# Routing of a two-layer trunk's mixture of experts rebuilt: router in strips, placement on GpSimd, expert rows fetched from DRAM, loops written out

## The reference

```
h = rms_norm(x);  q|k|v|value|gate = h @ w_in[layer]
attention: 8 heads, window 128, sinks;   conv: GLU, causal width 31, layer norm, silu
x = x + concat(attention, conv) @ w_out[layer]
h = rms_norm(x)
layer 0:  x = x + (silu(h @ w_gate) * (h @ w_up)) @ w_down          # width 2816
layer 1:  logits = h @ w_router                                      # 8 experts
          top 2 of 8 experts per token, softmax over the two logits
          x = x + sum over the two of weight * (silu(h @ w_gate[e]) * (h @ w_up[e])) @ w_down[e]   # width 3584
```

## Time and profile before

| | us |
|---|---|
| median of 3 runs | 1451.32 (1450.49 to 1452.38) |
| the profiled execution | 1446.28 |
| its span, first to last instruction | 1444.7 |
| PE busy | 1372.9 (95%) |
| DVE busy | 1076.3 (74%) |
| ACT busy | 915.5 (63%) |
| POOL busy | 53.7 (4%) |

### The profile page before, as it was taken

One profiled execution on the slowest core, in us unless ns is written; L12 is line 12 of the kernel. 1 busy time (PEld: TensorE's weight loads), 2 busy tenths in 40 slices (PEclk: granted clock), 3 DMA queues, 4 the chain that ended last, 5 costly groups with the idle time before them and its releaser, 6 DMA issues.

```text
span 1444.7 us, 19503 instructions
## 1 busy us (share of the span) xinstructions
PE 1372.9 (95%) x7441; PEld 1162.3 (80%) x7442; DVE 1076.3 (74%) x715; ACT 915.5 (63%) x731; POOL 53.7 (4%) x77
## 2 busy tenths in 40 slices
PE   6998999989988999999999999999999999999994
PEld 5867999979667888888788888878888888888883
DVE  5555444553656888888888898888888888888883
ACT  4564434344554777767776777767677677777771
POOL 3220000010200000000000000000000000000001
PEclk9999999989988999999999999999999999999997
DMA  9545655643624999999999999999999999999992
GB/s 323 157 138 170 202 174 181 211 145 108 206 88 145 368 342 363 393 370 336 372 378 339 376 386 340 343 392 368 339 373 392 343 372 390 358 355 382 390 343 103
DMA packets 198951, 428.10 MB, mean 296 GB/s; under 512 B 9304, under 2 KB 45392, under 8 KB 198864
## 3 DMA queue, kind: packets, MB, share of 16 engines
q1 hardware_dynamic: 195392, 416.71, 80.6%
q0 software_dynamic: 3472, 10.21, 1.9%
HBM read 415.42 MB, written 6.82 MB: 292 GB/s over the span
## 4 chain that ended last, share of the span: by engine, by line
PE 90%; DVE 4%; ACT 2%; DMA 1%; issue 1%; SPq 0%; POOL 0%; POOLq 0%; ACTq 0%; DVEq 0%
PE ps L1006 88%; DVE w_low L728 2%; PE ps L1209 2%; ACT w_high L514 1%; DMA raw<-in_w_in 1%; DMA raw<-y_slots,row_i 0%; PE ps L1029 0%; DVE hT_both L751 0%; SPq L344 0%; DVE h_td L744 0%; PE ps L1117 0%; DVE work_b L776 0%; DVE mx L769 0%; DVE h_td L833 0%; ACT sc L585 0%
## 5 line engine op out<-in xcount | busy, mean ns | idle before, releaser
L728 DVE TENSOR_TENSOR w_low<-raw,w_high 128x2048 fp32r<-128x2048 f32 x391 | 896.3, 2299 | 232.1 <-ACT w_high L514 231.6
L514 ACT ACTIVATE w_high<-raw 128x2048 fp32r<-128x2048 f32 x391 | 749.2, 1917 | 267.3 <-PE ps L1006 263.3
L1006 PE MATMUL ps<-w_high,hT_both 128*128 128x512 f32 (+1 forms) x1920 | 602.8, 391 | 13.2 <-issue 5.9
L1006 PEld LDWEIGHTS ps<-w_high,hT_both 128*128 128x128 f32 x1920 | 361.5, 189 | 86.9 <-issue 11.4
L1006 PE MATMUL ps<-w_low,hT_both 128*128 128x512 f32 (+1 forms) x960 | 372.2, 388 | 0.0
L1006 PE MATMUL ps<-w_high,act_both 128*128 128x512 f32 x1072 | 342.9, 391 | 1.8 <-DVE act_both L909 1.8
L1006 PEld LDWEIGHTS ps<-w_high,act_both 128*128 128x128 f32 x1072 | 202.2, 189 | 43.7 <-DVE act_both L909 2.1
L1006 PEld LDWEIGHTS ps<-w_low,hT_both 128*128 128x128 f32 x960 | 182.1, 190 | 35.0
L1006 PE MATMUL ps<-w_low,act_both 128*128 128x512 f32 x536 | 209.4, 391 | 0.0
L1006 PE MATMUL ps<-hT_both,w_high 128*128 128x256 f32 x960 | 177.5, 285 | 2.6 <-DVE hT_both L751 2.6
L1006 PEld LDWEIGHTS ps<-hT_both,w_high 128*128 128x128 f32 x960 | 152.1, 193 | 3.8 <-DVE hT_both L751 2.8
(11 more groups left out here) (184 smaller groups left out, 582.7 us busy)
## 6 DMA issues: line engine op xcount, KB each, us to landing
raw<-in_moe_w_gate SPq DMA_DIRECT2D x112, 1024.0 KB, 7.2
raw<-in_moe_w_up SPq DMA_DIRECT2D x112, 1024.0 KB, 7.2
raw<-in_moe_w_down SPq DMA_DIRECT2D x112, 1024.0 KB, 6.9
raw<-in_w_in SPq DMA_DIRECT2D x14, 1024.0 KB, 7.0
raw<-in_dense_w_gate SPq DMA_DIRECT2D x11, 1024.0 KB, 5.3
raw<-in_dense_w_up SPq DMA_DIRECT2D x11, 1024.0 KB, 5.4
raw<-in_dense_w_down SPq DMA_DIRECT2D x11, 1024.0 KB, 4.9
raw<-in_w_out SPq DMA_DIRECT2D x8, 1024.0 KB, 6.8
```

Source lines behind the costliest of these rows:

```text
L514: act.activation(w_part[0][:, s % PART_RING, :], raw[:, s % RAW_RING, :], ACT.Copy).then_inc(w_high_done, 1)
L728: dve.tensor_tensor(w_part[1][:, q, :], raw[:, r, :], w_part[0][:, q, :], ALU.subtract).then_inc(w_low_done, 1)
L1006: return pe.matmul(out_, lhsT, rhs, start=start, stop=stop, skip_group_check=True)
```

## The change

Five parts.

1. Norms 1, 2 and 3 treat block 1 in two halves of 512 columns. The last projection slot finishes the first half 6 matmuls early and says so (`half_projected`). ACT's sum of block 1 takes three activations before the root instead of one, and the weight slots that ACT rounded between the transposes are rounded after them. PE's first dense matmuls wait for the k chunks one pair at a time.
2. Router: `wr` is padded to 32 columns and is the stationary operand; 8 matmuls of 256 columns go to four column strips of the array, ACT copies the four partial results, and 2 matmuls with `mask` add them and turn them back. `route` loses an addition and two copies, the one-hot of experts 1 to 7 goes, and the weights' part (`weigh`) moves to DVE's end.
3. Placement runs on POOL (28 small instructions, each waiting for the one before). POOL writes `h_td` to DRAM, scatters the token numbers into a list with 4 indirect transfers, reads it back, and before each of experts 1 to 7 fetches its 128 rows (512 KB) to `xrows`. PE turns them by 8 transposes (`turn_rows`) where `gather` stood. Expert 0 is still gathered by matmuls.
4. The loop over expert pairs is written out on all engines.
5. The number of overflow passes is read at each engine's end.

```diff
-            with pe.Fori(0, NE // 2 - 1) as i:
-                expert_steps(S_MOE + 4, 0, 0, 2, True, i, (PAIR, 2 * EG, 2), lambda k: i * 2 + k)
-            expert_steps(S_MOE + 4 + (NE // 2 - 1) * PAIR, (NE - 2) * EG, NE - 2, 2, False, None, (0, 0, 0), lambda k: NE - 2 + k)
+            expert_steps(S_MOE + 4, 0, 0, NE, False, None, (0, 0, 0))
...
+            def turn_rows(i, per, e):
+                pe.wait_ge(rows_read, at(i, 16 * per, 16 * e))
+                for j in range(2):
+                    for k in range(4):
+                        last = pe.transpose(ps[:, (3, 6)[j], k * P:(k + 1) * P], xrows[:, (4 * j + k) * P:(4 * j + k + 1) * P], ident[:, :])
+                    last.then_inc(gathered, 1)
...
-                            gather(i, per_e, e + k // EG + 1, e_reg(k // EG + 1))
+                            turn_rows(i, per_e, e + k // EG + 1)
...
+            for i in range(2):
+                for g in range(4):
+                    last = mm(ps[QUAD * g:QUAD * (g + 1), 4, 0:S], wr[:, 4 * i + g, :], hT_plain[:, 4 * i + g, :], i == 0, i == 1)
+            last.then_inc(routed, 1)
+            pe.wait_ge(lgT_ready, 1)
             for t in range(NB):
-                for k in range(KC):
-                    last = mm(ps[:, 4, t * NE:(t + 1) * NE], hT_plain[:, k, t * P:(t + 1) * P], wr[:, k, :], k == 0 and t == 0, k == KC - 1)
-            last.then_inc(routed, 1)
+                last = mm(ps[:, 5, t * NE:(t + 1) * NE], lgT[:, t * P:(t + 1) * P], mask[:, 0:NE], True, True)
+            last.then_inc(summed, 1)
...
+            mm(ps[:, 4, NE:2 * NE], ones[:, :], sel[:, 0, :], False, True).then_inc(counted, 1)
+            mm(ps[:, 7, 0:NE], ones[:, :], sel[:, 0, :], True)
+            mm(ps[:, 7, 0:NE], ones[:, :], sel[:, 1, :], False, True).then_inc(counted, 1)
...
+                            if first and m == 0 and f == 0 and k % 2 == 0:
+                                pe.wait_ge(hT_low_done, 4 + k // 2 + 1)
...
+            act.wait_ge(routed, 1)
+            act.activation(lgT, ps[:, 4, 0:S], ACT.Copy).then_inc(lgT_ready, 1)
             act.wait_ge(zdiff_done, 1)
...
-            n_passes = passes_in_all(act)
             act.wait_ge(w_used, S_MOE + 2)
             act.activation(silu_t, ps[:, 0, :], ACT.Silu).then_inc(silu_done, 1)
...
-            place()
-            n_passes = passes_in_all(dve)
             dve.wait_ge(w_used, S_MOE + 4)
...
+                    act.wait_ge(x_added, 3 * (q - 1) + 2)
+                    act.activation(h_td[:, 1, 0:D // 2], xr[:, 1, 0:D // 2], ACT.Square, accum_out=ss[:, q, 1:2]).then_inc(sq_done, 1)
+                    act.wait_ge(sq_done, done + 2)
+                    act.activation(ss_half[:, q, 0:1], ss[:, q, 1:2], ACT.Identity, scale=1.0 / D, bias=eps_t[:, :]).then_inc(sq_done, 1)
+                    act.wait_ge(x_added, 3 * (q - 1) + 3)
+                    act.activation(h_td[:, 1, D // 2:D], xr[:, 1, D // 2:D], ACT.Square, accum_out=ss_half[:, q, 1:2]).then_inc(sq_done, 1)
+                    act.wait_ge(sq_done, done + 4)
+                    act.activation(rms[:, q, 1:2], ss_half[:, q, 1:2], ACT.Sqrt, scale=1.0 / D, bias=ss_half[:, q, 0:1]).then_inc(rms_done, 1)
...
+            for b in range(NB):
+                pool.wait_ge(h_done, 9 + 2 * b + 1)
+                pool.dma_start(h_dram[b * P:(b + 1) * P, :], h_td[:, b, :]).then_inc(h_stored, 16)
+            list_tokens()
+            place()
+            pool.wait_ge(h_stored, 16 * NB)
+            def fetch(e):
+                pool.wait_ge(gathered, 2 * e)
+                pool.indirect_dma_start(out=xrows[:, :], out_offset=None, in_=h_dram[:, :],
+                                        in_offset=bass.IndirectOffsetOnAxis(ap=slot_tok[:, e:e + 1], axis=0)).then_inc(rows_read, 16)
...
-            with pool.Fori(0, NE) as e:
+            for e in range(NE):
+                if e + 1 < NE:
+                    fetch(e + 1)
                 store(e)
+            n_passes = passes_in_all(pool)
```

More of the change, by code:

```diff
@@ L472, in conv, with link, add_up @@
                 pool.dma_start(gnorm[:, 1, :], ffn_norm_g[l].partition_broadcast(P)).then_inc(gain_loaded[1], 16)
+            steps = [0]
+            def link(ins):
+                steps[0] += 1
+                ins.then_inc(place_step, 1)
+                pool.wait_ge(place_step, steps[0])
+            def add_up(total, t):
+                for n in (4, 2):
+                    link(pool.tensor_tensor(t[..., 0:n], t[..., 0:n], t[..., n:2 * n], ALU.add))
+                link(pool.tensor_tensor(total, t[..., 0], t[..., 1], ALU.add))
@@ L534, in norm @@
                         act.activation(hT_plain[:, 2 * j:2 * j + 2, :], src, ACT.Copy).then_inc(hT_plain_done, 1)
+                if q > 0:
+                    for slot in slots:
+                        high(slot)
             def conv_copy(l, c):
@@ L889, in place, with weigh @@
+            def weigh():
                 dve.wait_ge(z_done, 1)
@@ L1179, in dense_down @@
                 a = [t[:, u, :].rearrange("p (f t) -> p f t", f=2) for t in act_part]
-                for t, f in order(stop):
-                    for hf in range(2):
-                        last = terms(ps[:, 4 + 2 * t + hf, :], a, (slice(None), f, slice(t * P, (t + 1) * P)), w, (slice(None), f, slice(hf * 512, (hf + 1) * 512)),
-                                     start and f == 0, stop and f == 1)
-                    if stop and (t, f) == (0, 1):
+                for t, f, hf in order(stop):
+                    last = terms(ps[:, 4 + 2 * t + hf, :], a, (slice(None), f, slice(t * P, (t + 1) * P)), w, (slice(None), f, slice(hf * 512, (hf + 1) * 512)),
+                                 start and f == 0, stop and f == 1)
+                    if stop and (t, f, hf) == (0, 1, 1):
                         last.then_inc(block0_projected, 1)
+                    if stop and (t, f, hf) == (1, 1, 0):
+                        last.then_inc(half_projected, 1)
                 last.then_inc(w_used, 1)
@@ L1210, in turn_act, with expert_steps @@
                 last.then_inc(act_turned, 1)
[L1212 removed]
+            def expert_steps(s, n, e, experts, following, i, pers):
                 per_s, per_n, per_e = pers
```

225 lines of the change are left out of this document (134 added, 91 removed).

## The result

| | kernel before | changed kernel |
|---|---|---|
| median, us | 1450.9 | 1409.8 (1408.2 to 1412.3) |
| ratio | | 0.972 (0.970 to 0.974) |
| profiled execution / its span | 1446.28 / 1444.7 | 1409.3 / 1407.6 |

The change gains 41 us. The prediction had 30.8, a time of 1420.5 and a low end of 1411: the sign was right, the size a quarter too small, and the time lies just under the range. 37.1 us of it show between the two profiled spans; the other 4 are that the profiled execution of before lay under its median and the one of after didn't.

What follows compares the result with a forecast made beforehand. The prediction took PE's own matmul stream in the 56 expert steps as the bound. Its terms, 18.7 + 6.0 + 2.7 + 0 + 3.7 + 1.0 - 0.3 - 1.0 = 30.8 us, gave 1420.5 us, range 1411 to 1435.

Steps and rivals of the forecast that it cites:

- rival 3: First gather and PE's start after norm 1 run at 2.4 GHz after shorter waits: 3 to 5 us more gained, 1416; chance 0.05.
- Gathers: Expert steps: seven gathers of 3.58 us each become 8 transposes of 0.9 us, saving 18.7 us.
- Loop: Expert-pair loop written out: PE's two stops of 3.0 us at the back edges go, 6.0 us, range 4 to 6.5.
- Norm 1: Before the dense stage: halves of block 1 and PE starting on the first subtraction save 2.7 us, bounds 1.5 and 4.
- Router, route, silu: Routing after layer 1: norm 3, router and route save 3.7 us together; waits before the first activations save 1.0 us.
- End: Before the last fetch: POOL reads the passes after the last store, 1.0 us lost, bounds 0.5 and 1.5.
- 1: Expert steps: transfers are the bound, with a ceiling below 381 GB/s, so the kernel gets slower, 1455.4; chance 0.05.
- 2: Expert steps: short gather step only partly won, DVE or transfers late, 7 to 15 us come back, 1428 to 1435; chance 0.11.
- 4: Placement beside expert steps: POOL instructions hold DVE's passes 1.7 us each, 33 us lost, 1453; chance 0.03.
- A: Experiments' theory: each term is about right; the missing gain is TensorE's clock, falling more often in the kernel before.
- B: Experiments' theory: the loop edges cost more than the two stops in the trace; 10 to 11 us for the loop alone.
- C: Experiments' theory: norms or router are worth more than their terms; norms alone 6 us or more, router 5 or more.

## Why the prediction was wrong

**The step that failed** is the clock of PE behind a stop. The sum has no term for it: the loop was priced at its two stops and at most 0.5 us more, norm 1 and the routing at the waits taken away, and a faster clock stood beside the sum as rival 3, with a chance of 0.05. The runs show that PE's matmuls often run at the low clock for a while after PE has stood still, and that taking such stops away gave back more than their length (in the traces 8.5 us for two stops of 3.0, and 1.9 us in the dense stage). Of the 10.3 us missed, by the means of the traces and rounded, 4.3 lie in the steps, 1.9 in the dense stage, 2.3 at the end, 1.6 in the routing and 0.3 at the start. Not all of it is shown to be the clock, and the paragraphs below say where.

**Gathers: right.** 8 transposes take 0.87 us (0.9 taken), the step 17.69, the seven save 18.8 (18.7). The thin reserve of DVE held in both traces of the changed kernel: inside the steps PE never waits for a pass.

**Loop: mis-sized.** Taken at the two stops, 6.0 us, with an upper bound of 6.5 for slow first matmuls. The stops are right, but after a stop the clock often falls: the two steps behind the edges together have 0, 4.5 and 1.5 us more than 2 x 16.61 in the three traces of before. In single steps it is 3 of these 6, and 1 of 2 each in the traces with only the norms changed (18.24 us) and with the loop put back. The prediction read the one trace that has none. With the slow first matmuls (2 x 0.26) the loop is worth 8.5 us on average in those traces; the chip gave 6.8 alone and 8.8 undone. This term failed most. The low clock also shows in the first step after the routing (17.94, 18.91 and 19.10 before; 17.91 and 16.61 changed), 1.4 us more by these means; six variants of the changed kernel have 18.2 there and one 16.6, so the usual gain may be half of that. 18.8 + 8.5 + 1.4 = 28.7.

**Norm 1: right, its consequence missed.** The mean of the traces is 2.7 us as predicted, but to hit it exactly is chance: the profiled trace alone gives 2.0, with its first transposes at a low clock (2.35 us for 10), and `w_out` to dense is 16.2 us in the second trace of the changed kernel and in six variants with the new norms, 3.2 under the 19.4 of before. The 1.8 us of starting on the first subtraction are there as they were put (0.70 us in place of 2.49). But PE now waits less and starts the dense stage at full clock: its first 10 us ran at 0.83 in the profiled trace of before and at 1.00 in that of the changed kernel, in these windows.

```profile
124.02:134.02 10.00, 10.00 (x71) 10.00 (x72) 4.38 (x3) 2.59 (x3) 0.00 (x0) 0.83 0.64 210
```

```profile
119.94:129.94 10.00, 10.00 (x83) 10.00 (x84) 7.60 (x6) 6.09 (x6) 0.00 (x0) 1.00 0.48 158
```

12 matmuls more fit into the same 10 us. The dense stage takes 182.0 to 182.3 us in all traces with the new norms and 183.3 to 184.6 in all with the old ones, so 1.9 us belong to the change. Rival 3 named this for PE's start after norm 1 and was given 0.05; the first gather, on which it counted as well, still ran at 0.69 and 0.73 (5.48 and 5.20 us, against 3.58 in the steps). It should have been a term with its own range, not a case apart.

**Norm 2: right**, 14.2 us from the last dense matmul to the next stage in both. **Norm 3: right**, 0.9 taken: from the start of `w_out`'s last slot to the router's matmuls it is 18.4 us in all three traces of before and 17.0 and 17.3 in the changed kernel, 1.2 us less. The strips then ran at the low clock, which took part of it back. **Router, route, silu**: 4.6 and 1.7 for 3.7 and 1.0. `route` gives 1.4 (1.5 taken). The rest is in part the clock's: before, the 16 matmuls took 4.5 to 7.0, and the first gather took 0.5 longer on average. (The prediction read that gather's clock as 0.50 from 2 of its 6.6 us; over the whole it was 0.56.)

**POOL: right.** 0.3 taken, and no loss shows: DVE's passes beside the placement keep their length. **End: size and sign.** The reading costs 0.8 as predicted (1.0). But the last slot takes 7.35 to 7.37 us in all three traces of before, at a granted clock of 0.77, and 5.75 in both of the changed kernel, at 1.00. It doesn't follow the change: the changed kernel with its fetches fourfold had 7.34 and with its gathers put back 7.37, and the kernel before with nothing but 64 matmuls at its head had 5.75. What decides it stays open, and so these 1.6 of the 41 us aren't shown to be the change's.

**The level.** The sum was made on a run that was itself 4.6 us below the median, and the difference was carried over to the changed kernel as if it belonged to both. For the larger part it was low-clock stretches behind the loop's edges that this trace lacked (0 against 4.5 and 1.5 us), and the change removes the edges. Between runs of the kernel before a mean granted clock lower by 0.001 goes with 1.0 us; 0.976 is usual for it and 0.983 for the changed kernel, so by an estimate some 7 of the 41 us are clock. The profiled time of 1415.5 that the sum gave stands against 1409.3.

**Rivals.** 1 fell, though 3% above the load the reserve was nearly gone. 2 and 4 didn't happen. Of the theories, A holds in kind, and B has a share: the edges are one of the places where the clock is lost. C has a small share in the norms (4.4 us alone and 5.7 undone, for 3.6 taken), which is for the most part the dense stage's clock; for the router it fell, within 3.8 us. The Trainium skill, "DMA: Bandwidth & Descriptors", section "Where 436 GB/s comes from", puts a core's HBM limit at about 358 GB/s. The same page of the Trainium skill, section "Measured (HBM→SBUF, 128 partitions, SWDGE, issued from GpSimd)", says that this is what each core gets when both cores of the HBM domain stream, and that its higher figures are of a core alone. This kernel uses one core, and the trace agrees with the second (392 GB/s over 910 us).

## What to carry to other kernels

A stall of PE costs its own length and then, in some runs, a stretch at half clock behind it: here 1.5 to 3 us behind a stop of 3.0. When a change removes stalls, add a term for the clock behind each, and take it from more than one trace; the profiled run here was faster than the median, and it lacked the stretches behind the edges. Where the clock is low in several stages in a row, a gain in one can be taken back in the next, so read the stages behind it as well. And a loop's edge has a price that moves with the code around it.

## What the runs showed of the hardware

- A loop edge stopped PE for 3.0 us once or twice, depending on 64 matmuls of code ahead of it; two stops at each edge and the clock behind them made that kernel 12 us slower than the median of before beside it (1463.0, 1451.0).
- Matmuls of zeros in the waits of the changed kernel raised the mean granted clock by only 0.002 (0.985 against 0.983) and didn't keep the first gather at full clock (6.76 us, 3.58 in the steps).
- Transfers to one core kept up 392 GB/s for 910 us, with ACT just beginning to wait (21.8 us in all).
- Small POOL instructions of 4 to 64 columns take 0.2 to 0.3 us alone and 2.1 to 2.3 beside a pass of DVE; the pass doesn't get longer by them (2290 ns).
